# Streaming encoder step on one core: scores first on VectorE, high parts first on ScalarE, and a new order of loads and splits around the output projections

## What is computed

```
h = rmsnorm(x, g_mix);  z = h @ w_in + b_in          # queries, keys, values, forget logits, two gates
ya = sliding-window attention with sinks (8 query heads, 2 key heads, head size 64)
yb = forgetting attention (8 heads): softmax(q k / 8 + c[t] - c[s]), causal; new tokens also see 2048 cached rows
merged = sigmoid(gate_a) * (ya @ w_oa) + sigmoid(gate_b) * (yb @ w_ob)
x = x + merged @ w_out
x = x + (silu(a) * u) @ w_down,   a, u = split(rmsnorm(x, g_ffn) @ w_gu)
y = rmsnorm(x, g_final);   keys, values and forget logs are stored too
```

## Time and profile before

| | us |
|---|---|
| median of 3 runs (1594.19 to 1595.05) | 1594.21 |
| the profiled execution's own time | 1592.57 |
| its span, first to last instruction | 1590.8 |
| TensorE busy (98%) | 1558.1 |
| weight loads of TensorE busy (92%) | 1463.9 |
| VectorE busy (65%) | 1033.2 |
| ScalarE busy (44%) | 702.0 |
| POOL busy (13%) | 202.0 |

### The profile page before, as it was taken

One profiled execution on the slowest core, in us unless ns is written; L12 is line 12 of the kernel. 1 busy time (PEld: TensorE's weight loads), 2 busy tenths in 40 slices (PEclk: granted clock), 3 DMA queues, 4 the chain that ended last, 5 costly groups with the idle time before them and its releaser, 6 DMA issues.

```text
span 1590.8 us, 26537 instructions
## 1 busy us (share of the span) xinstructions
PE 1558.1 (98%) x10156; PEld 1463.9 (92%) x10156; DVE 1033.2 (65%) x2033; ACT 702.0 (44%) x1376; POOL 202.0 (13%) x356
## 2 busy tenths in 40 slices
PE   8999999999999999998999999999999999999997
PEld 8999999999999999977998999999999999888886
DVE  6655654566656654474674877766777777679864
ACT  6335555566656644352443642222322223434453
POOL 3012221110100110031010000000221122110000
PEclk9999999999999999999999999999999999999999
DMA  7153333434445355878464423322444445766442
GB/s 210 33 161 107 128 115 113 121 104 114 131 117 140 94 170 152 222 243 226 122 200 138 132 75 115 110 82 82 125 145 144 158 150 199 246 216 191 139 137 81
DMA packets 194348, 226.25 MB, mean 142 GB/s; under 512 B 23832, under 2 KB 145210, under 8 KB 193704
## 3 DMA queue, kind: packets, MB, share of 16 engines
q1 hardware_dynamic: 167840, 138.71, 30.6%
q0 software_dynamic: 26384, 85.87, 16.1%
HBM read 166.76 MB, written 57.82 MB: 141 GB/s over the span
## 4 chain that ended last, share of the span: by engine, by line
PE 85%; DVE 7%; DMA 3%; ACT 3%; issue 2%; SPq 0%; DVEq 0%; ACTq 0%; POOLq 0%
PE ps L2492 24%; PE ps L2493 24%; PE ps L2494 23%; PE ps L2558 3%; PE ps L2578 2%; DMA w_raw<-in_w_out_dram 2%; PE ps L2600 1%; PE ps L2601 1%; DVE sprob L1718 1%; PE ps L2615 1%; PE ps L2809 1%; PE ps L2808 1%; DMA w_raw<-in_w_ob_dram 1%; DVE e_lo L2134 1%; PE ps L2655 1%
## 5 line engine op out<-in xcount | busy, mean ns | idle before, releaser
L2492 PE MATMUL ps<-h_hi,w_hi 128*128 128x384 f32 (+1 forms) x816 | 274.1, 336 | 1.3 <-DVE h_lo L1690 1.2
L2494 PE MATMUL ps<-h_hi,w_lo 128*128 128x384 f32 (+1 forms) x816 | 266.5, 327 | 0.0
L2493 PE MATMUL ps<-h_lo,w_hi 128*128 128x384 f32 (+1 forms) x816 | 266.2, 326 | 0.0
L2492 PE MATMUL ps<-t_hi,e_hi 128*128 128x272 f32 x704 | 202.7, 288 | 0.9 <-DVE silu L2149 0.9
L2493 PE MATMUL ps<-t_lo,e_hi 128*128 128x272 f32 x704 | 202.8, 288 | 0.0
L2494 PE MATMUL ps<-t_hi,e_lo 128*128 128x272 f32 x704 | 202.1, 287 | 0.0
L2492 PEld LDWEIGHTS ps<-h_hi,w_hi 128*128 128x128 f32 x816 | 153.4, 188 | 3.4 <-DVE h_lo L1690 1.5
L2492 PE MATMUL ps<-b_hi,e_hi 128*128 128x272 f32 x528 | 152.5, 289 | 2.2 <-DVE silu L2149 1.1
L2493 PEld LDWEIGHTS ps<-h_lo,w_hi 128*128 128x128 f32 x816 | 153.5, 188 | 0.5 <-issue 0.5
L2494 PEld LDWEIGHTS ps<-h_hi,w_lo 128*128 128x128 f32 x816 | 153.2, 188 | 0.0
L2493 PE MATMUL ps<-b_lo,e_hi 128*128 128x272 f32 x528 | 152.1, 288 | 0.0
(11 more groups left out here) (372 smaller groups left out, 3631.2 us busy)
## 6 DMA issues: line engine op xcount, KB each, us to landing
w_raw<-in_w_gu_dram SPq DMA_DIRECT2D x104, 256.0 KB, 3.4
w_raw<-in_w_in_dram SPq DMA_DIRECT2D x68, 256.0 KB, 3.5
zg_d<-stg POOLq DMA_DIRECT2D x28, 544.0 KB, 3.0
act_d<-act POOLq DMA_DIRECT2D x44, 272.0 KB, 2.8
s_d<-s_sum POOLq DMA_DIRECT2D x44, 256.0 KB, 3.4
f_raw<-s_d SPq DMA_DIRECT2D x44, 256.0 KB, 3.0
f_raw<-act_d SPq DMA_DIRECT2D x33, 256.0 KB, 2.7
w_raw<-in_w_out_dram SPq DMA_DIRECT2D x32, 256.0 KB, 3.6
```

The costliest lines, as they stand in the source:

```text
L2492: nc.tensor.matmul(out, l_hi, r_hi, start=start, stop=False)
L2493: nc.tensor.matmul(out, l_hi, r_lo, start=False, stop=False)
L2494: return nc.tensor.matmul(out, l_lo, r_hi, start=False, stop=stop)
```

## The change

Only orders change; no instruction is added or taken away. On each engine the count of instructions is the same.

```diff
-            turns_at[(130, 132, 133, 134)[c]].append(("cache", 0, c))
+            turns_at[(130, 131, 132, 134)[c]].append(("cache", 0, c))
...
-            load_x1(0)
             load_gates(0, 4)
             pool.wait_ge(o_ready, N_DUOS + 4)
+            load_outputs(pool, 1, 0)
             pool.dma_start(gffn_row[:, :], g_ffn.broadcast_to([P, D])).then_inc(gains_landed, 16)
-            for j in range(5, KD):
-                load_gates(0, j)
-            load_outputs(pool, 1, 0)
+            load_gates(0, 5)
             pool.wait_ge(sem("ab_lo"), 8)
             load_sums(pool, 1, 0)
-            load_gates(1, 0)
+            load_gates(0, 6)
...
             load_outputs(pool, 1, 1)
             load_sums(pool, 1, 1)
+            load_gates(0, 7)
+            load_x1(0)
             for x in range(2):
                 pool.dma_start(rooms[1]["ab_b"][:, x, :, 512:576].bitcast(F32), ots_d[x]).then_inc(sem("ab_landed11"), 16)
+            load_gates(1, 0)
...
                 if n + 1 < N_STREAM:
                     exp(n + 1)
+                turned_hi_part(n)
                 p = piece_at(n - 1)
                 if p is not None:
-                    evac(p, False)
-                turned_hi_part(n)
-                if p is not None:
-                    split_after(p)
+                    evac(p)
...
                 if s < 3:
                     turned_hi(("cache", s + 1, 2))
+                else:
+                    for k in range(2, 4):
+                        merged_in_hi(0, 0, k)
                 evac(d + 1)
...
                 else:
-                    for k in range(2, 4):
-                        merged_in_hi(0, 0, k)
+                    for k in range(4):
+                        merged_in_hi(0, 1, k)
                 evac(d + 2)
                 turned_hi(("ots", s))
-                if s == 3:
-                    for k in range(4):
-                        merged_in_hi(0, 1, k)
...
             for n in range(N_STREAM):
-                turned_lo_part(n)
                 if n + 2 < N_STREAM:
                     scores(n + 2)
+                turned_lo_part(n)
...
                     merged_in_scale(0, 0, (2, 3))
+                normalise(N_STREAM + s)
+                if s == 3:
+                    merged_in_scale(0, 1, (0, 1, 2, 3))
                     for k in range(4):
                         merged_in_lo(0, 0, k)
-                normalise(N_STREAM + s)
...
                 if s == 3:
-                    merged_in_scale(0, 1, (0, 1, 2, 3))
                     for k in range(4):
                         merged_in_lo(0, 1, k)
...
-                        pe.wait_ge(*((z_evac, N_DENSE) if k < 2 else (part_done, n_pieces)))
+                        pe.wait_ge(*((z_evac, N_DENSE - 1 + k) if k < 2 else (part_done, n_pieces)))
```

## The result

| | before | after |
|---|---|---|
| median of 4 runs, us | 1594.45 (1594.19 to 1595.05) | 1602.46 (1600.70 to 1605.83) |
| profiled execution, us | 1592.57 | 1605.83 |
| its span, us | 1590.8 | 1604.0 |

The ratio is 1.0053 (95% interval 1.0039 to 1.0068): 0.5% slower, where no change was forecast (1592.6, range 1586 to 1598). The profiled execution of the changed kernel is the slowest of its four, and that of before lies under its median, so the two executions differ by 13.3 us where the medians differ by 8.0. The traces tell where the time goes, the medians how much it is.

A forecast was written before the change was run, and what follows sets the result against it. TensorE is busy 98% of the span, so only its idle time can be won. -2.8 (stream) + 0.2 (cache chunks) + 1.0 (POOL's queue, end of attention's gain paid back) = -1.6 us: 1592.6 against 1594.21, range 1586 to 1598.

The forecast's parts named there:

- Stream, 2.8 gained: Attention stream: scores first and high parts first gain 3.6 us, less 0.5 and 0.3 lost, so 2.8 us.
- in window attention the next piece follows soon after: Window attention: emptying the piece behind the high part may lose 0 to 1.1 us; 0.3 us taken.
- 7 x 0.51 = 3.6: First seven heads: a weight load's 0.51 us wait on a score pass goes once in each, 3.6 us gained.
- netted 0.5: Later low parts delay transposes: two heads gain 0.35 us each, three lose 0.1, two lose 0.45; together 0.5 us lost.
- the prediction's own sign of being wrong: Stream from 280 to 556 us: the prediction is wrong if this has as much idle time as before.
- Cache chunks, 0.2 lost: Steps 130, 131, 132, 134: a 1.34 us wait goes, 1.5 us of new waits come; 0.2 us lost.
- End of attention, 2.3 gained: End of attention: the `ab_b` products start at 677.7, not 680.04, 2.3 us gained.
- POOL's queue, 1.0 lost beyond the 2.3: First merge: late gate tile 7 delays w_out, taking back the 2.3 us and losing 1.0 us more.
- SP loads four chunks of weights beside them, 5.1 us: Line ahead of gate tile 7: SP's four weight chunks, served in turn with POOL's loads, add 5.1 us.
- 32.3 us without a gap: From gate tile 4 to gate tile 7 the loads form an unbroken line of 32.3 us; tile 7 lands at 726.6.
- the mechanism I named: Merge: gate tile 7 lands behind attention loads, ScalarE waits for it, and w_out's first chunk starts at 730.2, not 719.7.
- Rival 4: Merge: gate tile 7 lands very late, at 3.4 us an attention load; slower, 1600.5 us; chance 14%.

The follow-up runs named there:

- stream_only: The kernel before with only the stream's two new orders, VectorE's and ScalarE's; 1597.92 us, ratio 1.0019.
- scores_only: The kernel before with only VectorE's new order in the stream, scores ahead of low parts; 1593.62 us, ratio 0.9995.
- end_only: The kernel before with only the new order at the end of attention and TensorE's split wait; 1590.97 us, ratio 0.9976.
- pool_only: The kernel before with only POOL's new list of loads; 1601.82 us, ratio 1.0045.
- wide_rows: pool_only with the w_oa and w_ob chunks read as 2,048-byte rows instead of 512, so other weights than the reference's; 1603.78 us, ratio 1.0062.
- mix: The kernel before with the new end of attention, scores first in steps 0 to 71, high parts first from step 72; 1589.45 us, ratio 0.9964.
- mix_whole: mix with the loads of the attention outputs made as 128 partitions instead of two of 64; 1585.76 us, ratio 0.9952.
- highs_fox: The kernel before with ScalarE's high parts ahead of emptying only from step 72 on (forgetting attention); 1593.18 us, ratio 0.9992.

## Why the prediction was wrong

- **Stream, 2.8 gained: wrong by 6.** stream_only lost 3.2. The step that failed is "in window attention the next piece follows soon after, and a fifth of a microsecond may be lost in some steps: 0 to 1.1 us, I take 0.3". With ScalarE's order alone 2.3 us are lost by 280 and 1.1 more by 320, and the transposes of tokens, which read the emptied piece and make most of it, weren't counted. The second part failed too. The 3.6 us of score waits did go, but "7 x 0.51 = 3.6" was a misreading that met the right total by luck: 0.51 us is the idle time of a weight load, the matmul behind it stood 0.27 us, and the 3.6 are the sum of all 12 waits. The waits on low parts came to 4.2 us in 9 places until 538 (and 1.8 in two behind it), where I netted 0.5. Two heads were priced as a gain, three as about even; in the trace each of the eight has a wait of 0.4 us or more. From 320 to 538 the changed kernel gained 0.6 us, not 3.1, and the prediction's own sign of being wrong came true: from 280 to 556 us TensorE idles 7.1 us, where it idled 5.8.
- **Cache chunks, 0.2 lost: too small.** TensorE waits 0.79 us at 544.4 and 0.96 at 554.5 for low parts of the last units and 0.49 for the chunk, 2.2 in place of 1.34 (two of the 11 waits on low parts are counted here); the same matmul comes 0.7 us later. These waits come from VectorE's order: scores_only, with the old steps, loses 1.0 there. No run had this step alone.
- **End of attention, 2.3 gained: right.** 2.4 in the trace, the wait at `ab_b` 0.5 us where under 1.2 was forecast, and end_only keeps 2.1.
- **POOL's queue, 1.0 lost beyond the 2.3: wrong, and the larger part.** pool_only costs 7.1 us. Two clauses failed. "SP loads four chunks of weights beside them, 5.1 us" counted these chunks as time in POOL's line, and never asked when they themselves land: 64 turns of 0.29 us (15 x 16 / 834) are 18 us a chunk beside a full POOL queue, an estimate, where two blocks of the merge, some 11 us, is what it has. The trace has 20.6 us for chunk 40 and 27.4 for chunk 41, which stood behind it. The same trace could have told, since the earlier trace rows give packets: 830 of SP beside 1412 of POOL. "32.3 us without a gap" failed too: gate tile 7 was issued at 723.3, after a wait of 13.2 us for the gating of block 5. From POOL's first packet of gate tile 4 at 697.9 it came in after 34.1 us, so that the 32.3 nearly fit is luck. It would have been late without that wait as well (wide_rows), so the mechanism I named was there, behind a nearer one.
- **Rivals.** Rival 4 had the sign and nearly the median (1600.5 for 1602.46), but its place, gate tile 7, held nothing in the changed kernel; it held once the weights were fast. That its time comes near is luck, then. The Trainium skill's rule that I cited (DMA: Bandwidth & Descriptors, "Queues, rings and completion order"), turns packet by packet, agrees with 834 against 835 packets. I used it to lengthen POOL's line only; read from SP's side it gives the answer.

By medians the parts are +7.1 (POOL), +3.2 (stream) and -3.8 (end): 6.5, against 8.0 for the whole.

## What to carry to other kernels

Where two queues share the DMA engines, count turns, not bytes, for each of them: a load of many short rows is late beside a queue of long ones, and the engine that splits it holds everything in its list behind it. When a load is late, look for a second line just behind it before pricing the cure: here the cure of the first alone gave nothing. An order that gains in one phase of a loop may lose in another; choose it by phase.

## What the runs showed of the hardware

- Two queues with work go one packet for one: 834 and 835 packets in 15 us, 884 and 885 in another kernel, with 3.8 KB a packet in the one and 0.5 KB in the other.
- A load into 64 partitions ran at half speed: 217 GB/s and 0.31 us a packet, against 407 GB/s and 0.18 us for the same data as one load into 128 (mix, mix_whole).
- Splitting a load by tokens did not make its packets shorter: of 4,096 or 4,608 B with it and without.
- Behind one and the same wait of 2.3 us TensorE's clock stayed at 2.4 GHz in some profiled runs (before, pool_only) and fell to 1.2 GHz in others (highs_fox, scores_only), worth 1.5 us.
